# A forgetting attention whose row minima move from VectorE to GpSimd, with GpSimd's other work placed between the row tiles

## The reference, cut to what matters

```python
c = jnp.cumsum(log_f, axis=1)                       # (B, T, H)
s = einsum('bhqd,bhkd->bhqk', q, k) * 64 ** -0.5
s = s + c[query] - c[key]
p = softmax(where(key <= query, s, -inf), axis=-1)
o_fox = einsum('bhqk,bhkd->bhqd', p, v)
o_fox = o_fox * silu(f_gate)
```

## Time and profile before

| what | value |
|---|---|
| median of three runs | 1272.03 us (1271.3 to 1273.73) |
| the profiled execution | 1274.2 us |
| its span from the first to the last instruction | 1272.5 us |
| mean granted PE clock | 0.981 of full speed |
| busy: PE / DVE / ACT / POOL | 1218.3 / 661.4 / 547.5 / 407.7 us |
| attention stage | from about 733 to 1085 us of the span |

### The profile page before, as it was taken

How to read it: one execution, slowest core, us unless ns; L and a number is a source line. 1 busy time by engine, 2 the same in 40 slices (tenths; PEclk the granted TensorE clock), 3 DMA queues, 4 the chain that set the end, 5 groups by cost and what they waited for, 6 DMA issues and landing times. The chain is left out here.

```text
span 1272.5 us, 18832 instructions
## 1 busy us (share of the span) xinstructions
PE 1218.3 (96%) x6256; PEld 997.8 (78%) x6256; DVE 661.4 (52%) x1496; ACT 547.5 (43%) x1116; POOL 407.7 (32%) x512
## 2 busy tenths in 40 slices
PE   5999999999999999998999989989999998899997
PEld 5998877888777777777888767877787787688886
DVE  3763435101333334423555369878898887544443
ACT  5553133013444442213555357777787777211111
POOL 3553631122333333323334143252225315111110
PEclk9999999999999999999999989999999999799999
DMA  8884132223333334435444493235045201443431
GB/s 317 265 288 130 62 96 97 72 82 115 101 107 107 107 107 132 130 120 155 131 150 141 125 229 121 91 97 140 9 150 114 70 10 57 192 149 149 149 146 70
DMA packets 106820, 161.57 MB, mean 127 GB/s; under 512 B 12148, under 2 KB 62324, under 8 KB 105124
## 3 DMA queue, kind: packets, MB, share of 16 engines
q1 hardware_dynamic: 103920, 151.46, 38.1%
q10 hardware_dynamic: 2616, 8.66, 1.7%
q0 software_dynamic: 192, 0.33, 0.2%
HBM read 102.67 MB, written 57.74 MB: 126 GB/s over the span
## 5 line engine op out<-in xcount | busy, mean ns | idle before, releaser
L1038 PE MATMUL tok_tps<-h_T,tok_slot 128*128 128x512 f32 x2088 | 489.8, 392 | 0.0
L1038 PEld LDWEIGHTS tok_tps<-h_T,tok_slot 128*128 128x128 f32 x2088 | 389.6, 188 | 82.6 <-issue 2.3
L2104 PE MATMUL out_yps<-out_w,out_mix 128*128 128x512 f32 x768 | 178.3, 395 | 7.9 <-POOL out_mix L2153 7.1
L2104 PEld LDWEIGHTS out_yps<-out_w,out_mix 128*128 128x128 f32 x768 | 146.1, 191 | 40.4 <-ACT out_w L2170 8.5
L1867 ACT ACTIVATE fox_pT<-fox_tps 128x512 fp32r<-128x512 f32 x240 | 124.1, 529 | 80.8 <-PE fox_tps L1797 77.4
L1923 DVE TENSOR_TENSOR fox_pT<-fox_tps,fox_pT 128x512 fp32r<-128x512 f32 x240 | 143.9, 606 | 20.3 <-ACT fox_pT L1867 18.3
L1912 DVE TENSOR_SCALAR_CACHE_REDUCE fox_prob<-fox_sps 128x512 f32<-128x512 f32 (+1 forms) x240 | 141.5, 605 | 11.4 <-PE fox_sps L1788 9.3
L1797 PE MATMUL fox_tps<-all_ident,fox_prob 128*128 128x128 f32 x816 | 133.2, 276 | 4.6 <-ACT fox_prob L1859 3.0
L1797 PEld LDWEIGHTS fox_tps<-all_ident,fox_prob 128*128 128x128 f32 x816 | 101.7, 141 | 31.9 <-ACT fox_prob L1859 6.3
L1859 ACT ACTIVATE fox_prob<-fox_prob,fox_nm 128x512 f32<-128x512 f32 (+7 forms) x96 | 114.8, 1196 | 5.5 <-POOL fox_qb L1567 5.3
L1814 PE MATMUL fox_ops<-fox_pT,fox_v 128*128 128x512 f32 (+3 forms) x384 | 112.2, 375 | 1.6 <-ACT fox_pT L1867 1.6
(11 more groups left out here) (199 smaller groups left out, 1671.0 us busy)
## 6 DMA issues: line engine op xcount, KB each, us to landing
scr_split<-cg_stage SPq DMA_DIRECT2D x64, 256.0 KB, 2.9
open_raw<-in_w_cols SPq DMA_DIRECT2D x22, 512.0 KB, 4.4
open_raw<-in_x SPq DMA_DIRECT2D x16, 512.0 KB, 6.6
tok_xT<-in_x_cols SPq DMA_DIRECT2D x16, 512.0 KB, 6.2
scr_gates<-cg_stage SPq DMA_DIRECT2D x32, 256.0 KB, 2.5
outw_mix<-scr_mix SPq DMA_DIRECT2D x16, 512.0 KB, 4.4
out_x<-in_x SPq DMA_DIRECT2D x16, 512.0 KB, 3.5
out<-out_o ACTq DMA_DIRECT2D x15, 512.0 KB, 2.6
```

What stands on the lines that cost most here:

```text
L1038: mm = nc.tensor.matmul(cps[u % 2], w[j % 2][a_][:, kk, :], hT[b_][:, kk, c * CH:(c + 1) * CH], start=(kk == 0 and r == 0), stop=(kk == KT ...
L2104: mm = nc.tensor.matmul(yps[t % 2][:, c, :], mix[t % 2][a][:, kk, :], w[b][:, kk, c * CH:(c + 1) * CH], start=(kk == 0 and n == 0), stop=( ...
```

## The change

The minimum over the quarters leaves DVE. POOL folds it instead, in `least`: for a row tile with more than one unit, each unit from the second on is compared with the result so far by one `tensor_scalar` with ALU.min on one column; for a row tile of one unit, one such instruction copies it. A fold waits for the unit's negation, and from the third unit on for the fold before it. The last one of a row tile increments `maxed`. The four of the first turn are made in a new prologue on POOL, which stands behind its fills.

POOL's other work gets fixed places between the row tiles of the next turn. In turn t, q being the row tile's number in order of time: behind row tile 0 the gate product of turn t-2 (now a function `gate_scale` of its own), behind row tile 1 the output product of turn t-2, behind row tile 2 the diagonals of turn t. Each is followed by a wait for its own end. After the last turn come the products of the last two turns. Before, the products of turn t-1 were made during turn t. On DVE `invert` moves behind the first `pt_low` of the turn.

```diff
@@ vector @@
                         if c == g:
-                            dve.wait_ge(negated, S.at(n + 1))
-                            nc.vector.tensor_reduce(nm[t % 2][:, i:i + 1], nmax[t % 2][:, i, 0:c + 1], AX.X, ALU.min
-                                                    ).then_inc(maxed, 1)
...
                         ahead, steps = plan(t, last)
-                        invert(t)
                         for m, (u, made, _) in enumerate(steps):
                             for a in made:
                                 negate(ahead[a], s1 + a, t + 1)
                             pt_low(u, k0 + m)
+                            if m == 0:
+                                invert(t)
                             if ends(t, m):
                                 add(t - 1)
@@ gpsimd @@
+                    def least(u, n, t):
+                        e, g, i, c, w = u
+                        if 0 < g and c == 0:
+                            return
+                        best, this = nmax[t % 2][:, i, max(c - 1, 0):max(c - 1, 0) + 1], nmax[t % 2][:, i, c:c + 1]
+                        to = nm[t % 2][:, i:i + 1] if c == g else this
+                        pool.wait_ge(negated, S.at(n + 1))
+                        if c > 1:
+                            pool.wait_ge(folded, F.at(folds_before(t) + (QT - 1 - i) * (g - 1) + c - 1))
+                        pool.sem_inc(pool_goes, 1)
+                        nc.gpsimd.tensor_scalar(to, this, best, None, ALU.min).then_inc(maxed if c == g else folded, 1)
...
+                    if prologue:
+                        for n, u in enumerate(score_units(*turns[0])):
+                            least(u, n, 0)
+                        pool.wait_ge(maxed, QT)
+                        return
                     for t in range(n_turns):
-                        diagonals(t)
-                        if t:
-                            gated_output(t - 1)
+                        ahead = plan(t, last)[0]
+                        tiles = len(ahead) // QT
+                        for q in range(QT):
+                            for a in range(q * tiles, (q + 1) * tiles):
+                                least(ahead[a], at_turn(t + 1)[0] + a, t + 1)
+                            if ahead:
+                                pool.wait_ge(maxed, E.at(QT * (t + 1) + q + 1))
+                                pool.sem_inc(pool_goes, 1)
+                            if q == 0 and t >= 2:
+                                gate_scale(t - 2)
+                                pool.wait_ge(gate_scaled, G.at(t - 1))
+                                pool.sem_inc(pool_goes, 1)
+                            if q == 1 and t >= 2:
+                                gated_output(t - 2)
+                                pool.wait_ge(gated, G.at(t - 1))
+                                pool.sem_inc(pool_goes, 1)
+                            if q == 2:
+                                diagonals(t)
+                    pool.wait_ge(maxed, E.at(QT * (n_turns + (not last))))
+                    pool.sem_inc(pool_goes, 1)
+                    gate_scale(n_turns - 2)
+                    gated_output(n_turns - 2)
+                    gate_scale(n_turns - 1)
                     gated_output(n_turns - 1)
+                    pool.wait_ge(gated, G.at(n_turns))
+                    pool.sem_inc(pool_goes, 1)
+                round_(0, False, prologue=True)
                 rounds(pool, round_)
```

More of the change, by code:

```diff
@@ L1659, in forgetting_attention @@
         rps = k.ps("rps", [P, CH])
-        names = ("pool_goes gate_scaled gate_loaded0 gate_loaded1 scored negated maxed expd transposed pt_hi pt_lo "
+        names = ("pool_goes gate_scaled gate_loaded0 gate_loaded1 scored negated folded maxed expd transposed pt_hi pt_lo "
                  "weighed inverted ones_made rinv_hi rinv_lo diag_done spread low_done added scaled gated sp_goes").split()
-        (pool_goes, gate_scaled, gate_loaded0, gate_loaded1, scored, negated, maxed, expd, transposed, pt_hi, pt_lo,
+        (pool_goes, gate_scaled, gate_loaded0, gate_loaded1, scored, negated, folded, maxed, expd, transposed, pt_hi, pt_lo,
          weighed, inverted, ones_made, rinv_hi, rinv_lo, diag_done, spread, low_done, added, scaled, gated,
@@ L1669, in forgetting_attention, with folds_before @@
         n_turns = len(turns)
+        def folds_before(t):
+            return sum(QT * max(g - 1, 0) for _, g in turns[:t])
         def at_turn(t):
@@ L1914, in negate @@
                                                 ).then_inc(negated, 1)
-                        if c == g:
-                            dve.wait_ge(negated, S.at(n + 1))
-                            nc.vector.tensor_reduce(nm[t % 2][:, i:i + 1], nmax[t % 2][:, i, 0:c + 1], AX.X, ALU.min
-                                                    ).then_inc(maxed, 1)
                     def pt_low(u, n):
@@ L1964, in _, with round_ @@
                 pool.wait_ge(ones_made, 1)
-                def round_(r, last):
-                    G = Ring(r, n_turns)
+                def round_(r, last, prologue=False):
+                    S, G, E = Ring(r, n_scores), Ring(r, n_turns), Ring(r, QT * n_turns)
+                    F = Ring(r, folds_before(n_turns))
+                    def least(u, n, t):
[9 more added lines that the diff above has]
+                        nc.gpsimd.tensor_scalar(to, this, best, None, ALU.min).then_inc(maxed if c == g else folded, 1)
                     def diagonals(t):
@@ L1988, in diagonals, with gate_scale @@
                         pool.sem_inc(pool_goes, 1)
-                    def gated_output(t):
+                    def gate_scale(t):
                         b = t % 2
@@ L1995, in gated_output @@
                                                 ).then_inc(gate_scaled, 1)
+                    def gated_output(t):
+                        b = t % 2
                         pool.wait_ge(gate_scaled, G.at(t + 1))
```

## The result

The changed kernel takes **1335.58 us** (median of 4 runs, 1335.09 to 1336.22) against 1272.88 us of the kernel before beside it on the same chip (4 runs, 1271.3 to 1273.84). The ratio is 1.0496, with a 95% interval of 1.0483 to 1.0509. That is 62.7 us slower. The forecast was 27.0 us slower, and the range ended at 1316. The profiled execution has a span of 1333.6 us and a mean PE clock of 0.963 (before: 1272.5 us and 0.981). Among the runs reported further down, one of 2012.5 us of the kernel before with 24 counting instructions, with a granted clock of 0.558, was in a slow state and is left out of its median and ratio.

The account below looks back on a forecast made before the run. DVE, without a gap while scores are made, was taken as the bound, its 96 minima costing 18 us. Late starts and tiles less a 4.2 us gain summed to +27.0 us: 1299.0 us, own range 1291 to 1306, 80% range 1279 to 1316.

Parts of the forecast that it names:

- the start, +6.8: Start of the attention stage: the first four minima stand behind POOL's fills, delaying the next scores by 6.8 us, once.
- the fold's own time: One minimum step on POOL was taken as 0.27 us, between bounds of 0.20 and 0.48 us.
- the mechanism: Folds stand behind POOL's blocks of 1.5, 1.5 and 3.0 us, so ACT's exponentials wait 20 to 30 us in all.
- turns 6 and 7: Short turns at a round's end: late tile 3, +2.8 us three times and +2.9 us twice, 14.2 us together.
- followed by a wait for its own end of about 0.2 us: After each gate product, output product and diagonals, POOL was said to wait about 0.2 us for its own result.
- turns 1 and 2, "+0.9" and "+0.2 and no gain": Tile 3 late by 0.9 us in turn 1 (2.7 us in all), 0.2 us in turn 2 (0.6 us in all).
- turn 0: Round's first turn: tile 3's exponential late behind the diagonals, +1.6, +1.4 and +2.4 us by round, +5.4 us together.
- the loop's return: Jump back between rounds: ACT's 2.2 us stand stays; POOL does not stand, at most +0.9 us, not in the sum.
- the gain of 0.7 us in turns 3 and 4: Long turns where POOL's blocks fit between tiles: relieving DVE saves 0.7 us each, six times, -4.2 us.
- Rival 4: The start costs as said but the gain in turns 3 and 4 fails: +4.2 us, within the forecast's own range.
- A low clock: New 3 us stands of PE may lower its clock: up to +10 us or nothing, none in the sum.
- Rival 3: Worse case: the fold at its upper price and PE's clock down after stalls, +27 + 7 + 5, 1311 us; chance 20%.

Follow-up runs that it names:

- 24 counting instructions: Kernel before with 24 semaphore instructions that compute nothing added behind each gate product on POOL: 1274.48 us, ratio 1.0013.
- Bodies of 127, 205 and 223 instructions: POOL's loop body in: kernel before (127); changed kernel, all minima on DVE (205), 1276.6 us; kernel before, 12 idle semaphore instructions per gate product (223), 1271.5 us.
- the split stand: Changed kernel with the first turn's four minima back on DVE: 1328.46 us, ratio 1.0431; two folds split POOL's stand into 7.50 and 6.79 us.
- bodies of 319 and 397: POOL's loop body in the kernel before with 24 counting instructions (319), 1274.48 us, and in the changed kernel (397), 1335.58 us.
- these three: Changed kernel with the first turn's minima on DVE, diagonals behind tile 3 and rounds written out, all together: 1283.47 us, ratio 1.0074.

## Why the prediction was right and wrong

- **Right: the start, +6.8.** 6.4 in the timeline, 7.1 measured by undoing it.
- **Right: the fold's own time and the mechanism.** 280 ns against 0.27 us, 1.8 times the minimum on DVE (156 ns, another instruction for the same step). Tile 3 behind the diagonals is the largest single cause, ACT passes the delay on, and turns 6 and 7 cost most among the turns, as forecast. Behind them comes turn 2 (+4.7) and not turn 5 (+2.4).
- **Wrong: "followed by a wait for its own end of about 0.2 us".** That was read from the earlier trace rows, where one semaphore instruction stands between two products. In the changed order there are two, and with the loop two register instructions: 0.37 us at each block, 0.42 ahead of the cast with its three. Tile 0 to tile 3 in turn 7 takes 8.31 us instead of 7.3. Here turns 6 and 7 cost 19.4 us instead of 14.2.
- **Wrong: turns 1 and 2, "+0.9" and "+0.2 and no gain".** No stretch has turn 1 by itself. The stretch of turn 2 became 1.6 us longer in each round, and with the diagonals behind tile 3 it was 18.7 us, under the 19.0 of before. So the lateness was that of the diagonals, in a turn where I had tile 3 ready just when ACT wants it.
- **Wrong, and the largest miss: turn 0 and "the loop's return".** The sum had +1.4 for turn 0 and said that the 2.2 us of ACT stay. Measured: 17.0 us more at this boundary. The step that failed is "POOL, now short, does not stand at the return in this trace; no run shows a longer one", with the most that it would cost put at "+0.9 us" and none of it in the sum. POOL stood 14.99 us there. I gave the rule of the Trainium skill's page "Advanced Engine Details and Errata", section "ISA Cache", a price of 0.9 us by putting ACT's 2.2 us in POOL's place. The runs agree with that page of the Trainium skill in part. Bodies of 127, 205 and 223 instructions do not stand, and the split stand, with its two packets, fits two fetches. But two lines of 256 hold 512, and bodies of 319 and 397 stood. By the 16 KB for 256 instructions in that section of the Trainium skill, a packet of 8 KB, as this trace has them, would be 128 instructions (an estimate from that page's figures); two of those would hold 256, between 223 and 319. A body that touches a third line of 256 would explain it as well, and no run decides between the two. And ACT's stand is no measure for POOL's: ACT went on at 876.07 us, before the first of SP's loads (877.95), POOL came back behind it (its last product ends at 878.87). I had counted SP's loads in the change only for their own lateness and not for what they do to another transfer.
- **Wrong: the gain of 0.7 us in turns 3 and 4.** With nothing late on POOL the gain is 0.0 to 0.2 us in nearly every turn. That DVE "runs without a gap" was taken for the bound. PE had no gap either, and I had set that aside as partly modelled.
- **The rivals.** Rival 4, the gain fails, came true inside a worse case. A low clock is there (0.50 at the return), but it lies in the stand, and what it adds to it is not separated. Rival 3 named a dearer fold, which did not come; its 1311 us were still too low: no case had a stand of POOL over 2.2 us, nor the longer waits behind each block.

By size: 62.7 us = 7.1 (start) + 29.6 (diagonals ahead of tile 3) + 15.4 (the loop, as the remainder; the kernel before has 4 of it in its own loop) + 10.6 (not repaired by these three: in turns 6 and 7 and at the boundaries). With both kernels written out that last part is 14.1 us, since the kernel before gains its 4 us as well.

## What to carry to other kernels

An engine with long blocks and idle time is no place for a small step that others wait for: what counts is what stands ahead of it on that engine and the wait behind each block, not its busy share. Before relieving an engine without gaps, look whether another has none either. In a hardware loop, count each engine's instructions in the body, with waits and register instructions: here 223 on POOL did not stand at the return and 319 did. Where there is a stand, see what waits behind it, and issue no big loads just then, or write the rounds out.

## What was not expected of the hardware

- POOL's stand at the return: 4.91 us with the DMA engines quiet, and 14.99 us (7.50 and 6.79 in the split case) with SP's loads in flight at a DMA share near 1. The packets of the instruction queue that start in the stand are 7.8 us apart with the loads and 2.2 us without, though each takes 0.6 us or less. That POOL's instructions wait behind the loads is inferred from this and from the run with the loads held back; no run shows it directly.
- ACT and DVE, with 346 and 302 instructions in their bodies in the changed kernel (DVE had 334 before), stand only 1.42 and 2.46 us at the same return. Why so much less than POOL, whose quiet stand is 4.91 us, is not settled.
- A POOL instruction behind another one's result starts 0.18 to 0.20 us after it with one semaphore instruction between them in the list, 0.30 us with two, 0.37 us with two and two register instructions, which the loop needs, and 0.42 us with three and one register instruction.
